# Differential attention: combining the two exponential tiles on VectorE and turning one tile with plain transposes, the first reciprocal applied at the way out of the bank

## What is computed

```
def diff_mixer(lat, ctx, lam_params, lam_init, norm_g, cos, sin, need_ctx):
    ...
    lam = jnp.exp(jnp.sum(lp[0] * lp[1])) - jnp.exp(jnp.sum(lp[2] * lp[3])) + lam_init
    ...
# for 4 heads, query blocks of 128 tokens, key width 64, value width 128:
p1 = softmax(q1 @ k1.T * scale);  p2 = softmax(q2 @ k2.T * scale)
p = p1 - lam * p2
out = p @ v          # then an RMS norm over the 128 values of a head
```

## Time and profile before

| | |
|---|---|
| time, median of 3 runs | 3960.57 us (3959.37 to 3961.09) |
| the profiled execution, first to last instruction | 3959.2 us |
| TensorE busy | 3737.7 us, 94% of the span |
| VectorE busy | 2437.2 us, 62% |
| ScalarE busy | 1663.1 us, 42% |
| mean granted TensorE clock | 0.971 of full speed |
| block of layer 0 | from about 927 to 1068 us |
| block of layer 1 | from about 2968 to 3069 us |

### The profile page before, as it was taken

The page is one execution under the profiler, slowest core; times in us unless marked ns, Lnnn a source line. Parts: engine busy times, 40 slices in busy tenths (PEclk is TensorE's granted clock), DMA queues, the critical chain, the costliest instruction groups (busy, mean ns, idle before and its releaser), DMA issues. The chain is left out here.

```text
span 3959.2 us, 66093 instructions
## 1 busy us (share of the span) xinstructions
PE 3737.7 (94%) x23706; PEld 3306.4 (84%) x23706; DVE 2437.2 (62%) x4777; ACT 1663.1 (42%) x2976; POOL 749.3 (19%) x302
## 2 busy tenths in 40 slices
PE   8999999799889999999999999999698899999998
PEld 7788799686569999887899999888586899998887
DVE  6542343375439789655567898555555397896555
ACT  4444032233234444445544444444433344444544
POOL 4554064000028200000076000000000382000000
PEclk9999999898899999999999999999897999999999
DMA  6668655220035444555544444555330354445554
GB/s 249 235 211 278 226 167 173 95 91 33 11 102 170 143 145 150 172 194 174 193 155 159 146 148 155 191 191 191 109 110 1 124 169 141 147 149 177 194 192 148
DMA packets 171119, 614.70 MB, mean 155 GB/s; under 512 B 18688, under 2 KB 22144, under 8 KB 170880
## 3 DMA queue, kind: packets, MB, share of 16 engines
q1 hardware_dynamic: 170880, 611.44, 46.1%
HBM read 610.31 MB, written 1.05 MB: 154 GB/s over the span
## 5 line engine op out<-in xcount | busy, mean ns | idle before, releaser
L2061 ACT ACTIVATE ring_hi<-ring 128x1024 fp32r<-128x1024 f32 x785 | 832.5, 1061 | 564.9 <-DMA ring<-in_peer_v 507.4
L1944 PE MATMUL bank<-H_r,ring_hi 128*128 128x256 f32 x3264 | 948.4, 291 | 49.8 <-POOL ring_r L1929 25.3
L1945 PE MATMUL bank<-H_r,ring_hi 128*128 128x256 f32 x3264 | 927.7, 284 | 0.0
L1946 PE MATMUL bank<-H_r,ring_r 128*128 128x256 f32 x3264 | 927.6, 284 | 0.0
L1944 PEld LDWEIGHTS bank<-H_r,ring_hi 128*128 128x128 f32 x3264 | 630.4, 193 | 57.5 <-issue 27.9
L1945 PEld LDWEIGHTS bank<-H_r,ring_hi 128*128 128x128 f32 x3264 | 631.0, 193 | 0.0
L1946 PEld LDWEIGHTS bank<-H_r,ring_r 128*128 128x128 f32 x3264 | 629.9, 193 | 0.0
L1929 POOL TENSOR_TENSOR ring_r<-ring,ring_hi 128x1024 fp32r<-128x1024 f32 x159 | 433.5, 2740 | 725.2 <-ACT ring_hi L2061 724.6
L276 POOL TENSOR_TENSOR ring_r<-ring,ring_hi 128x1024 fp32r<-128x1024 f32 x128 | 308.5, 2414 | 1005.6 <-ACTq L304 662.9
L1997 PE MATMUL bank<-ring_hi,w_high 128*128 128x512 f32 x1536 | 476.6, 391 | 10.0 <-DVE ring_r L2283 9.9
L2001 PE MATMUL bank<-ring_hi,w_low 128*128 128x512 f32 x1536 | 473.9, 390 | 0.0
(11 more groups left out here) (339 smaller groups left out, 5281.5 us busy)
## 6 DMA issues: line engine op xcount, KB each, us to landing
ring<-in_peer_u SPq DMA_DIRECT2D x384, 512.0 KB, 3.3
ring<-in_peer_v SPq DMA_DIRECT2D x384, 512.0 KB, 3.3
ring<-in_w_in SPq DMA_DIRECT2D x135, 512.0 KB, 3.3
arena<-in_ada SPq DMA_DIRECT2D x96, 512.0 KB, 5.7
ring<-in_w_f SPq DMA_DIRECT2D x72, 512.0 KB, 4.2
ring<-in_w_br SPq DMA_DIRECT2D x24, 512.0 KB, 4.5
ring<-in_w_q SPq DMA_DIRECT2D x24, 512.0 KB, 3.3
ring<-in_w_out SPq DMA_DIRECT2D x16, 512.0 KB, 3.3
```

The costliest lines, as they stand in the source:

```text
L1944: pe.matmul(o, hi[:, k], x_hi_[:, kt, :], start=(kt == 0), stop=False)
L1945: pe.matmul(o, hi[:, k], x_lo_[:, kt, :], start=False, stop=False)
L1946: mm = pe.matmul(o, lo[:, k], x_hi_[:, kt, :], start=False, stop=(kt == KT - 1))
L2061: act.activation(ring_hi[:, m % NH, :], ring[:, (n0 + m) % NS, :], ACT.Copy).then_inc(a_hi, 1)
```

## The change

The two diagonals are gone. VectorE forms one number per row, minus lambda times the first row sum times the second reciprocal, and adds the second exponential tile, times this number, onto the first in place (a `scalar_tensor_tensor` over all keys of the item). TensorE then transposes that one tile, 128 columns at a time. What is still missing, the first reciprocal, is multiplied in when the output of `attend` leaves bank 7. `lam_ident` and `diag` are no longer kept. The wait in `shares` for the matmuls that read the old diagonal becomes a wait for `keep(n - 2)`, which reads the same `stats`.

```diff
-            lam_ident = A.take(P)
             E = A.take(2, 2, 2 * T)
             htmp = A.take(4, ML_D)
-            diag = A.take(2, 2, P)
...
                         for k in range(keys_of(n) // P):
-                            o, c = bank[6][:, k * P:(k + 1) * P], slice(k * P, (k + 1) * P)
-                            pe.matmul(o, E[:, n % 2, 0, c], diag[:, n % 2, 0, :], start=True, stop=False)
-                            mm = pe.matmul(o, E[:, n % 2, 1, c], diag[:, n % 2, 1, :], start=False, stop=True)
+                            c = slice(k * P, (k + 1) * P)
+                            mm = pe.transpose(bank[6][:, c], E[:, n % 2, 0, c], ident)
                         mm.then_inc(pt_ps, 1)
...
                     def shares(n):
-                        st = stats[:, n % 2, :]
+                        nk, st = keys_of(n), stats[:, n % 2, :]
                         dve.wait_ge(a_exp, 2 * (n + 1))
                         if n >= 2:
-                            dve.wait_ge(pt_ps, n - 1)
+                            dve.wait_ge(v_o, n - 1)
                         link(dve.reciprocal(st[:, 6:8], st[:, 2:4]))
-                        for s in range(2):
-                            w = dve.tensor_scalar(diag[:, n % 2, s, :], lam_ident if s else ident, st[:, 6 + s:7 + s],
-                                                  None, ALU.mult)
-                        w.then_inc(v_p, 1)
+                        link(dve.scalar_tensor_tensor(st[:, 5:6], st[:, 2:3], nlam, st[:, 7:8], ALU.mult, ALU.mult))
+                        first, second = E[:, n % 2, 0, 0:nk], E[:, n % 2, 1, 0:nk]
+                        dve.scalar_tensor_tensor(first, second, st[:, 5:6], first, ALU.mult, ALU.add).then_inc(v_p, 1)
...
                         dve.wait_ge(o_ps, n + 1)
-                        dve.tensor_copy(yd[:, qt, h * P:(h + 1) * P], bank[7][:, 0:P]).then_inc(v_o, 1)
+                        dve.tensor_scalar(yd[:, qt, h * P:(h + 1) * P], bank[7][:, 0:P], stats[:, n % 2, 6:7], None,
+                                          ALU.mult).then_inc(v_o, 1)
...
-                    link(dve.tensor_scalar(lam_ident, ident, nlam, None, ALU.mult))
```

## The result

The changed kernel is slower: 3987.18 us median of 4 runs (3978.11 to 3995.55) against 3960.65 us (3959.37 to 3961.09), a ratio of 1.0065 with a 95% interval of 1.0049 to 1.0081. The forecast was 3950 with a range up to 3963; it missed in sign.

A forecast was written before the change was run, and what follows sets the result against it. No engine bounds either block throughout; the chain changes hands, with TensorE's turning often last. Savings of -15.3 us and +4.5 for late clock returns gave -10.8, so 3948.4 against the 3959.2 span, about 3950 as median; range 3941 to 3963.

The forecast's parts named there:

- TensorE's records and their prices: Turning: long items go from 16 records to 4, short from 8 to 2, at 0.11 us each at full clock.
- the addition on VectorE: In `shares`: the second tile added onto the first, 0.75 us long with 512 columns, 0.48 with 256.
- the output step: Copy from the bank becomes a multiplication by a number per row, at 24 places: 0, bound +1 us.
- VectorE's side of the change: Longer `shares` at k = 1: +0.7 us in layer 0 (four short), +1.3 in layer 1 (three long).
- what item 0 gave up: Layer 1, first item: ScalarE's 1.49 us wait goes, but its exponentials come 0.44 later, leaving -1.0 us.
- the one-column operation: In `shares`, between the reciprocal and the addition: priced at 0.18 us.
- The saving at an unchanged clock: Sum over both blocks: -9.9 us in layer 0 and -5.4 in layer 1, together -15.3.
- I take two of six, +4.5: Six clock returns at turnings, three per layer; two come late by one `values`, 2.2 us each: +4.5 us.
- rival 3: Turning at k = 2: transposes don't bring the clock back; 3966, up to about 4000; chance 0.06 to 3968.5, 0.08 above.
- the row of 24 transposes at 0.50: Last part of the block: TensorE busy 5.64 of 6.30 us, clock still 0.50; cited for transposes not raising it.
- Rival 2: Both blocks: VectorE's longer `shares` moves to the front, savings capped tighter; -4.9 us, no change; chance 0.22.
- Rival 4: Both blocks: half-clock savings come through and VectorE's waits close, 26 us at full clock, some 3934; chance 0.06.

The follow-up runs named there:

- e2: Changed kernel with two matmuls against the identity in place of each transpose, as many TensorE records as before: 3965.59 us, ratio 1.0001.
- e5: Changed kernel with every transpose issued four times into the same place: 3959.45 us, ratio 0.9999.
- e12: Changed kernel with unread matmuls in TensorE's waits (3, 5 and 2 in layer 0; 2, 4 and 0 in layer 1): 3939.02 us, ratio 0.9936.
- e8: Kernel before with unread matmuls in TensorE's waits (3, 5 and 0 in layer 0; 2, 5 and 2 in layer 1): 3954.23 us, ratio 0.9981.
- e7: Changed kernel with unread matmuls in TensorE's waits (3, 6 and 3 in layer 0; 2, 9 and 2 in layer 1): 3949.83 us, ratio 0.9966.
- e9: The changed kernel run again, unaltered, on another chip beside the kernel before: 3986.37 us, ratio 1.0049.
- e10: Changed kernel with transposes issued four times only for the long items at k = 2 of layer 0: 3964.99 us, ratio 0.9997.
- e6: Changed kernel with every transpose issued twice: 3969.54 us, ratio 1.0020.
- e3: Kernel before, diagonals still made, but each 128 keys turned by one transpose of the first tile, second tile left out: 3975.24 us, ratio 1.0025.
- e11: Changed kernel with transposes issued four times only for the long items at k = 3 of layer 0: 3980.30 us, ratio 1.0044.
- e1: Changed kernel with one matmul against the identity in place of each transpose: 3966.86 us, ratio 1.0018.
- e4: Kernel before, diagonals still made, but only the first matmul of each pair issued, second tile left out: 3966.78 us, ratio 1.0002.

## Why the prediction was wrong

**Right, step by step.** TensorE's records and their prices; where the blocks start and end; the addition on VectorE; the output step at its upper bound; the self-wait on `keep(n - 2)` at nothing. VectorE's side of the change costs 1.9 and 2.5 us by e2, 0.8 and 2.4 by e5, where the terms were +0.7 and, with what item 0 gave up, about +1.7; the one-column operation (219 ns) was under-sized, and the output step (350 ns), taken at 0, came at its bound. The saving at an unchanged clock, -15.3 in the sum, was not measured. With the clock held up in both, e12's layer 0 block is 124.2 us and e8's 135.7, 11.5 us apart, and layer 1's 4.8 (the sum had -9.9 and -5.4); but they are of different chips, clocks and fillings. e7, on e8's chip and with more added, is only 3.3 us under e8 in layer 0 and 5.5 over it in layer 1. The saving is of the right sign where the filling is not too long; its size stays open.

**The step that failed** is the clock: "I take two of six, +4.5; the bounds are 0 and +13." The mechanism was named, and rival 3 named its place, "the turning at k = 2, which brought the clock back"; it had 0.14, and it is what happened. What was wrong with the step:

- A late return was priced at the length of one `values`. There is no such limit. The return that came in the first head's turning at k = 2 before was missed, the clock was still at 0.50 for the 28 us behind that turning (958.6 to 986.8), and the whole stretch at half clock was 53.3 us, in which TensorE was busy 92% of the time. Even the upper bound of the six, +13, was passed: layer 0's block alone went from the 131.7 us of the sum (141.6 - 9.9) to 166.6, 34.9 us more (33.7 in e9), where the term had 4.5 for both layers. Layer 1, 95.0 by the sum, measured 102.6 and 98.9: 7.6 and 3.9 us more. If the saving was over-sized, a part of these us is that and not the clock; the runs don't separate the two, but e10's 139.0 us with 48 records more shows that most of layer 0's is the clock.
- The count of the returns was low by one: in layer 1 the clock rises at about 2980.8, 2991.0, 3035.4 and 3055.9 before, four times in or right behind a turning, so it was seven in all. At 2.2 us each that changes little.
- The argument against rival 3, no turning from 1020.5 to 1027.6 and the clock at 1.00, is about holding a clock that is up. It says nothing about what brings it up. From 959.6 to 974.8 the changed kernel does nearly the same work without a pause, at 0.50, and stays there. The two rows together show that nearly the same steps hold the clock at 1.00 in one state and don't lift it in the other.
- The rival's reason was wrong, though: not the transposes as such (e5, e6), but that the turning has a quarter of its records. My doubt about the row of 24 transposes at 0.50, that it did not tell them from the idle time, was justified.

**The other rivals.** Rival 2, VectorE moves to the front: no, e2. Rival 4, more than forecast: no; e12 comes near its 3934, but with matmuls added that the rival did not have. The time came in rival 3's interval from 3966 to 4000.

**What stays open.** e3's two groups of runs differ in the granted clock (0.962 or 0.963, and 0.958 or 0.959), so they are groups of the clock. Why it is up for longer in one run than in another, with the same instructions, is not shown; e3 was profiled in one run, of the upper group. That the changed kernel scatters more than the kernel before is not shown either: on the first chip it was 17 us over four runs against 2, on e9's 20 over six against 16 over 17. In e11 the clock returned at about 963 and 1032, where the row of 16 transposes had only begun, so that row did not bring it back there; what did, I can't say. What in the records of `values` and `products` fails to lift the clock, their 65 columns, the 64 rows of the product or the short pauses, was not separated.

## What to carry to other kernels

Before TensorE work is cut out of a latency-bound stretch with an unsteady granted clock, look for what the engine did just before each rise of the clock: that work may be paying for everything behind it, and its price is then not its own length. Halving the records of one step cost up to 0.2% here (e1, e4, e6) and quartering them 0.25 to 0.65% (e3, e9 and the first result); putting 48 useless transposes back at one place got it back. A wait that an in-order TensorE has anyway can be filled with matmuls nobody reads: with the fill sized to the wait the same change turned from +0.5% into -0.6% against the kernel before, of which the fill alone is worth some 0.2% there (e8), and with too much of it the fill itself became the chain (layer 1 of e7). And a lower granted clock is not by itself a longer block: four profiles of the changed kernel's layer 1 (the first, e9, e10, e11) have 98.8 to 103.0 us at 0.61 to 0.63, around the 100.4 us at 0.77 of before.

## What the runs showed of the hardware that I had not expected

- TensorE can be busy 15.15 of 15.20 us at 1.2 GHz and not be granted 2.4 GHz, with records of 128 x 65, 64 x 512, 4 x 512 and 128 x 128; with 16 transposes of 128 x 128 in a row it rose right behind them in each of e10's four heads (at about 957, 988, 1018 and 1049 us). Such a row is not the only thing that does it: e11's clock rose without one before it.
- 32-bit transposes and matmuls count alike for the granted clock of the block, to 0.01 in layer 0 in two pairs (0.78 and 0.78, 0.69 and 0.70) and to 0.02 in layer 1 (0.75 and 0.75, 0.69 and 0.71).
- The clock is also a matter of history: nearly the same steps (the later window has four transposes among them) run at 1.00 when it is up (7.1 us from 1020.5 before) and at 0.50 when it is down (15.2 us from 959.6 after).
